# A two-block transformer layer on one core: loads in another order, own banks for two chunks, weigh products spread

## The reference, cut to what matters

```python
def first_block(x, mem, ...):
    h = rms_norm(x, g_mix_pre[l])
    proj = h @ w_in[l]                       # q, k, v of 8 + 8 heads of 64, forget gates
    o_f = fox_attention(...)                 # causal, with a decay from the forget gates
    o_c = chunked_rel_attention(...)         # chunks of 64, 8 to the left, relative bias
    mix = jnp.concatenate([rms_norm(o_f, ..), rms_norm(o_c, ..)], axis=-1) @ w_out[l]
    x = x + rms_norm(mix, g_mix_post[l])
    ca = memory_cross_attention(rms_norm(x, ..), rms_norm(mem, ..), w_mem_q[l], w_mem_kv[l], w_mem_o[l])
    x = x + rms_norm(ca, g_mem_post[l])
    x = x + rms_norm(swiglu(rms_norm(x, ..), w_gate_up[l], w_down[l]), g_ffn_post[l])

def second_block(x, c, ...):
    cond = jax.nn.silu(c)
    for l in range(2):
        ada = cond @ ada_w[l] + ada_b[l]     # shift, scale and gate, twice
        h = modulate(rmsnorm(x, norm_g[l, 0]), sh1, sc1)
        y = mlstm_mixer(h, ...) if l == 0 else mla_mixer(h, ..., *shared_kv)
        x = x + g1[:, None, :] * rmsnorm(y, norm_g[l, 1])
        h = modulate(rmsnorm(x, norm_g[l, 2]), sh2, sc2)
        y = sqrelu_mlp(h, mlp_w1[l], mlp_w2[l])
        x = x + g2[:, None, :] * rmsnorm(y, norm_g[l, 3])
```

## Time and profile before

| | |
|---|---|
| runs | 2259.11, 2255.01, 2258.81 us |
| median | 2258.81 us |
| profiled execution | 2257.02 us |
| its span in the trace | 2255.2 us |
| mean granted clock | 0.973 |
| PE busy | 2127.5 us (94%) |
| DVE, ACT, POOL busy | 1087.3, 876.0, 958.2 us |

### The profile page before, as it was taken

One profiled execution on the slowest core, in us unless ns is written; L12 is line 12 of the kernel. 1 busy time (PEld: TensorE's weight loads), 2 busy tenths in 40 slices (PEclk: granted clock), 3 DMA queues, 4 the chain that ended last, 5 costly groups with the idle time before them and its releaser, 6 DMA issues.

```text
span 2255.2 us, 27272 instructions
## 1 busy us (share of the span) xinstructions
PE 2127.5 (94%) x9534; PEld 1693.5 (75%) x9534; DVE 1087.3 (48%) x1672; ACT 876.0 (39%) x1442; POOL 958.2 (42%) x489
## 2 busy tenths in 40 slices
PE   5899889889999999889998999999999999999997
PEld 3777678677788888667766688888777776888886
DVE  2753661422465556655364543343565425343435
ACT  4224774344422222424265423222465544232332
POOL 2335676353344444423313344444435533444443
PEclk8999999999999999999999999999998999999999
DMA  4671034112254454347102223323222012233322
GB/s 172 211 266 45 20 116 146 57 37 75 66 179 159 156 171 164 112 159 262 65 1 69 67 84 95 101 93 95 91 78 72 1 47 66 88 98 93 100 95 84
DMA packets 66607, 234.38 MB, mean 104 GB/s; under 512 B 7136, under 2 KB 8416, under 8 KB 66400
## 3 DMA queue, kind: packets, MB, share of 16 engines
q1 hardware_dynamic: 66528, 233.33, 31.7%
HBM read 231.20 MB, written 2.10 MB: 103 GB/s over the span
## 4 chain that ended last, share of the span: by engine, by line
PE 72%; issue 13%; DVE 5%; ACT 5%; POOL 4%; DMA 1%; POOLq 0%; SPq 0%; DVEq 0%; ACTq 0%
PE bank L776 22%; PE bank L777 21%; PE bank L778 21%; POOL WL L658 3%; PE bank L883 2%; PE bank L868 1%; PE bank L950 1%; DVE H L2006 1%; DVE bank L2012 1%; PE bank L1017 1%; DVE Y L2248 0%; ACT Y L1556 0%; PE bank L889 0%; PE bank L1051 0%; PE bank L1276 0%
## 5 line engine op out<-in xcount | busy, mean ns | idle before, releaser
L658 POOL TENSOR_TENSOR WL<-stage,WH 128x1024 fp32r<-128x1024 f32 x272 | 660.6, 2429 | 1028.2 <-ACT WH L1378 1028.1
L1378 ACT ACTIVATE WH<-stage 128x1024 fp32r<-128x1024 f32 x272 | 288.2, 1060 | 918.6 <-PE bank L778 881.0
L776 PE MATMUL bank<-H,WH 128*128 128x512 f32 x1324 | 522.0, 394 | 25.3 <-DVE H L2006 11.8
L777 PE MATMUL bank<-H,WH 128*128 128x512 f32 x1324 | 519.4, 392 | 0.0
L778 PE MATMUL bank<-H,WL 128*128 128x512 f32 x1324 | 518.9, 392 | 0.0
L776 PEld LDWEIGHTS bank<-H,WH 128*128 128x128 f32 x1324 | 250.8, 189 | 84.9 <-issue 30.6
L778 PEld LDWEIGHTS bank<-H,WL 128*128 128x128 f32 x1324 | 250.8, 189 | 52.6
L777 PEld LDWEIGHTS bank<-H,WH 128*128 128x128 f32 x1324 | 250.9, 190 | 52.1 <-issue 0.5
L776 PE MATMUL bank<-HID,WH 128*128 128x512 f32 x688 | 268.8, 391 | 5.4 <-DVE Y L2248 5.4
L2248 DVE TENSOR_TENSOR Y<-bank,Y 128x512 f32<-128x512 f32 x344 | 226.3, 685 | 97.3 <-PE bank L778 96.4
L778 PE MATMUL bank<-HID,WL 128*128 128x512 f32 x688 | 268.4, 390 | 0.0
(11 more groups left out here) (394 smaller groups left out, 3075.8 us busy)
## 6 DMA issues: line engine op xcount, KB each, us to landing
stage<-panels SPq DMA_DIRECT2D x296, 512.0 KB, 3.5
apiece<-ada SPq DMA_DIRECT2D x112, 512.0 KB, 4.3
RAW<-panels SPq DMA_DIRECT2D x18, 512.0 KB, 3.8
x<-xT SPq DMA_DIRECT2D x4, 1024.0 KB, 7.8
outT<-x SPq DMA_DIRECT2D x8, 256.0 KB, 2.0
Y<-bias SPq DMA_DIRECT2D x1, 1024.0 KB, 4.8
V<-memT SPq DMA_DIRECT2D x2, 512.0 KB, 4.5
con<-cons SPq DMA_DIRECT2D x1, 517.0 KB, 6.7
```

The lines of the kernel that those rows point to most:

```text
L658: pool.tensor_tensor(low_of(p, slot), stage[:, slot, :], high_of(p, slot).bitcast(F32), ALU.subtract).then_inc(s_split, 1)
L776: pe.matmul(out, wh, rh, start=start, stop=False)
L777: pe.matmul(out, wh, rl, start=False, stop=False)
L1378: act.activation(high_of(p, slot), stage[:, slot, :], ACT.Copy).then_inc(s_hisplit, 1)
```

## The change

1. Start. x comes in three parts, the ones (a part of `con`) right behind the first of them with a semaphore of their own, and panels 0 and 1 before the rest of the constants, the condition and the gate weights. PE's mean square waits for the ones alone. ACT's high halves of panels 2 and 3 stand between its high chunks of x. SiLU of the condition and its table loads stand after the evacuation of chunk 0, and DVE waits for them after the low half of chunk 0.
2. SP's order of panels and pieces in w_in, a_in and the feed forward: panels first (`pieces_ahead`), pieces behind.
3. `own_bank`: chunks 2 and 3 of w_in, mem_q and a_in go to the banks ST and AD.
4. Self attention: weigh products by the table `WEIGHED_AT` over seven steps; ACT's outputs and value stage at steps 6 and 7, POOL's low half of the values at 7, four norm steps by one later.
5. mlp0 and mlp1: even groups in G[0] and G[1], odd ones in ST and AD, with waits relaxed by one group.
6. `warm(AD, 12)`, twelve matmuls whose result isn't used, ahead of the mla attention.
7. mem_q: high halves of its first panels between the squares of x, those of the extra ones between the high chunks.
8. Feed forward on DVE: pieces 0 to 3 right behind the first hidden values, then 4 of them behind each group's additions, and none in the last loop half.

```diff
+X_PARTS = [range(0, 2), range(2, 4), range(4, 8)]
+WEIGHED_AT = [[(0, 0), (0, 1)], [(1, 0), (1, 1)], [], [(0, 2)], [(1, 2)], [(0, 3)], [(1, 3)], []]
...
+        def own_bank(name, c):
+
+            return [ST, AD][c - 2] if name in JOINT and c in (2, 3) else G[c % 2]
...
+            for at, part in enumerate(X_PARTS):
+                sp.dma_start(x[:, part.start:part.stop, :],
+                             xT[part.start * P:part.stop * P, :].rearrange("(c p) t -> p c t", p=P))\
+                    .then_inc(s_x[at], 16)
+                if at == 0:
+                    sp.dma_start(con[:, 0:CON["mask"]], cons[:, 0:CON["mask"]]).then_inc(s_ones, 16)
             sp.dma_start(vec[:], vecs).then_inc(s_const, 16)
+            for slot in range(2):
+                sp.dma_start(stage[:, slot, :], panels[slot]).then_inc(s_stage[slot], 16)
...
+            def pieces_ahead(p0, q0, n):
 
                 with sp.Fori(0, n) as i:
                     for j in range(4):
-                        load_panel(i * 4 + (p0 + j), j % 2)
                         load_piece(i * 8 + (q0 + 2 * j), 0)
                         load_piece(i * 8 + (q0 + 2 * j + 1), 1)
+                        load_panel(i * 4 + (p0 + j), j % 2)
...
-            plain(p0, p0 + 12)
-            load_piece(q0, 0)
-            load_piece(q0 + 1, 1)
-            with sp.Fori(0, 4) as i:
-                for half in range(2):
-                    for j in range(6):
-                        load_panel(i * 12 + (p0 + 12 + 6 * half + j), j % 2)
-                        if j < 4:
-                            load_piece(i * 8 + (q0 + 2 + 4 * half + j), j % 2)
-            for j in range(6):
-                load_panel(p0 + 60 + j, j % 2)
-                if j < 4:
-                    load_piece(q0 + 34 + j, j % 2)
-            load_piece(q0 + 38, 0)
-            load_piece(q0 + 39, 1)
+            plain(p0, p0 + 6)
+            with sp.Fori(0, 10) as i:
+                for j in range(6):
+                    load_panel(i * 6 + (p0 + 6 + j), j % 2)
+                    if j < 4:
+                        load_piece(i * 4 + (q0 + j), j % 2)
             plain(p0 + 66, p0 + 68)
             p0, q0 = PANEL0["a_in"], 80
-            plain(p0 + 2, p0 + 4)
-            load_piece(q0, 0)
-            load_piece(q0 + 1, 1)
-            with_pieces(p0 + 4, q0 + 2, 3)
-            end_pieces(p0 + 16, q0 + 26, 8)
+            plain(p0 + 2, p0 + 6)
+            pieces_ahead(p0 + 6, q0, 3)
...
-                        if s >= 12 and s % 8 in (4, 5):
+                        if s >= 12 and s % 8 in (6, 7):
                             out(2 * (s // 8 - 1) + s % 2)
...
+                            if not gated and not (isinstance(g, int) and g < 2):
+                                pe.wait_ge(sm["hidden"], g * 2 + j - 3)
...
+            warm(AD, 12)
...
+                if c == 0:
+                    act.wait_ge(s_c, 16)
+                    act.activation(cond[:], cond[:], ACT.Silu).then_inc(s_cond, 1)
+                    load_ln_exp()
...
+                if m in (2, 5):
+                    act.wait_ge(s_used, RING1 - 1 + (m - 2) // 3)
+                    extra_high("mem_q", (m - 2) // 3)
...
-                hidden(0, 0)
-                with dve.Fori(0, (groups - 1) // 2) as i:
+                def two_groups(i, pieces_then):
                     hidden(i * 2 + 1, 1)
                     add(i * 2)
-                    pieces(i, 0)
+                    pieces(i, range(4, 8))
                     hidden(i * 2 + 2, 0)
                     add(i * 2 + 1)
-                    pieces(i, 1)
+                    if pieces_then:
+                        pieces(i, range(8, 12))
...
+                hidden(0, 0)
+                pieces(0, range(0, 4))
```

More of the change, by code:

```diff
@@ L978, in attention @@
                             score_pair(s + 4)
-                        if s >= 8 and s % 8 < 4:
-                            n, piece = 2 * (s // 8 - 1) + s % 2, s % 8 // 2 * 2
-                            weigh(n, piece)
-                            weigh(n, piece + 1)
+                        if s >= 8:
+                            for h, piece in WEIGHED_AT[s % 8]:
+                                weigh(2 * (s // 8 - 1) + h, piece)
                         continue
@@ L989, in attention @@
                 if name == "self":
-                    for half in range(2):
-                        for n in (heads - 2, heads - 1):
-                            weigh(n, 2 * half)
-                            weigh(n, 2 * half + 1)
+                    for step in WEIGHED_AT:
+                        for h, piece in step:
+                            weigh(heads - 2 + h, piece)
                 else:
@@ L1055, in feed_forward @@
                 sm = ff[name]
-                banks = [G[0], G[1], ST, AD] if gated else [G[0], None, G[1], None]
                 per = 2 if gated else 1
@@ L1589, in feed_forward @@
                 sm = ff[name]
-                banks = [G[0], None, ST, None] if gated else [G[0], None, G[1], None]
                 per = 2 if gated else 1
@@ L1663, in _ @@
             act.wait_ge(s_eps, 1)
-            squares("x", xc, lambda m: act.wait_ge(s_x if m < 4 else s_x2, 16))
+            squares("x", xc, lambda m: [act.wait_ge(s_x[at], 16) for at, part in enumerate(X_PARTS) if part.start == m])
             panel_high(0, 0)
@@ L1667, in _ @@
             root("x")
+            act.wait_ge(s_ones, 16)
             act.wait_ge(s_const, 32)
-            extra_high("w_in", 0)
-            high("x", scaled_in, hh, lambda m: col("zero"))
-            extra_high("w_in", 1)
+            for m in range(KC):
+                high_chunk("x", m, scaled_in, hh, lambda m: col("zero"))
+                if m in (4, 6):
+                    extra_high("w_in", (m - 4) // 2)
             act.activation(identr[:], ident, ACT.Copy)
```

103 lines of the change are left out of this document (55 added, 48 removed).

## The result

The changed kernel took 2283.4 us (median of 4 runs, 2280.5 to 2294.8) against 2259.0 of the kernel before (2255.0 to 2262.4): a ratio of 1.0118, with an interval of 1.0080 to 1.0157. It is 1.2% slower. The forecast was 2273, the range 2246 to 2296. The profiled execution after took 2284.55 us with a span of 2282.8, 27.6 more than the span of before.

The account below looks back on a forecast made before the run. TensorE, busy 94% of the span, bounds the kernel, so only its idle time or clock matters. Terms 59 - 7 - 7 - 9.6 + 4 - 8 - 9.3 - 8 = +14 on 2257.0 gave 2271, 2273 as median; range 2246 to 2296.

Parts of the forecast that it names:

- the feed forward's order: Feed forward loop: pieces behind later panels delay the down products, 4.2 us idle ten times (42) plus 17 of clock: +59.
- its tail: Feed forward's last loop half has no pieces, so 5.42 us of idle time and 1.6 of clock go: -7.
- a_in: Projection a_in: four waits and clock go (-11.8), two stalls of 5.9 and 7 with clock come (15.9): net +4.
- Rival (d): Projections: idle moves from chunks 2 and 3 to 4 and 5, only the start gains; 2285, no separate chance.
- mem_q: Projection mem_q: earlier high halves take away 7.33 us of idle time and 2.3 of clock: -9.6.
- The chain in the feed forward: With T the start of group h+1's products: late piece, hidden product T+20.9, low half T+25.8, down products needing it at T+21.76.
- Rival (a): Feed forward: the order costs nothing, as the hidden product may start as late as T+16.7; 2214, chance 0.13.
- The start: Before w_in: early ones and panels let the first products start at about 21.1 instead of 29.86 us: -8.7.
- w_in: Projection w_in: at best -26.8 including the start, but VectorE's remaining work returns 14.2 and some 5 of clock: -7.
- the MLPs: The two ungated MLPs: a second pair of banks ends a 2.80 us wait in each, with clock: -9.3 together.
- the self attention: Self attention: spread weigh products and moved steps cover about 1.3 us in each of six to seven units: -8.
- mla: Before mla attention: twelve extra products fill 2.39 us idle; the 20.48 us half-clock stretch, not all TensorE-bound, shortens: -8.

Follow-up runs that it names:

- The run at T+15.7: Changed kernel with the feed forward's pieces on SP one panel earlier (piece 4h+j behind panel 6h+5+j): 2222.9 us, ratio 0.9831.

## Why the prediction was right, and where it was not

**Sign and size.** Slower was right, and the measured 2283 lies 10 above the 2273 and inside the forecast's own 2260 to 2288. The reason given first is the right one: the feed forward's order, named as +59 with its tail at -7, measured +54.0 together. The spans differ by 27.6 us where the sum had 14. Nearly all of the difference is one term, a_in, which came out 15.8 higher; that the time still fell into the range is owed to the width of the range. Rival (d), the idle time moving to chunk 4, gave 2285, nearer than the forecast. That is what happened in a_in. But its +12 is the gain of a_in alone; the 9.6 of mem_q, which by its words should be gone too, is not in the sum, and mem_q kept its gain. So its nearness is luck.

**The chain in the feed forward** held step by step. In the group shown: issue of the panel T+14.8 (T+14.8 forecast), hidden product T+20.9 (T+20.9), down products T+25.7 (T+25.8 to 26.0). The ten idle times are 3.75 to 4.40 us, 39.4 in all (42). What it rested on was a row of the kernel before that showed the time at which the very panel is issued, and the fact that the hidden product of before stood directly behind its last piece with no room. Each of the ten idle times had its own slow stretch, and none stands in the loop without them. That bears out the rule of the Trainium skill (page "TensorE: Matmul & The Clock Gate", section "HAM oscillation — how this bites in real kernels"), by which the clock falls in every tile that waits. Their price was mis-sized low: seven stretches are 3.41 us long and three 6.83, 44.4 in all. 54.0 less the idle time of 39.4, plus the 5.4 of the tail, leaves about 20 for the clock net of the tail's own, and I had 17 less 1.6.

**Rival (a)** put the point from which the order decides at T+16.7 for the hidden product. The run at T+15.7 has no idle time, and the change at T+20.9 has 3.8, which fits a threshold at about T+17; no run lies between the two.

**The start** gave 10.8 instead of 8.7: the products start at 19.05, since the panels were split sooner than my 21.1, for which the prediction gives no working. No run takes the start alone.

**w_in** was right in its sum (+1.4 behind the start) and in the step that the work of VectorE is not gone. Its parts were not: idle times of 5.6, 1.7, 1.0, 2.7 and 2.2 us stand at chunks 4, 6, 8, 9 and 12, 13.2 in all where I had 14.2. Chunks 4, 8 and 12 were named, 6 and 9 not, and the sizes are other ones, so the sum is right in part by luck.

**mem_q, the MLPs, the self attention** came within 2 us. In each MLP the idle time of 2.8 us and its slow stretch are gone; the pair of banks is the only one of the eight changes that touches these stages, but no run takes it alone. The cause for mem_q was wrong in the prediction: "earlier high halves" were named, and the run with own banks alone shows that the banks do it. What is missing to 9.6 is an idle time of 1.7 us that the prediction didn't have, at 391.68, among the products of the memory values, where TensorE waits for VectorE's `acc`. One of 1.6 to 1.8 us stands there in every kernel built on the change, and in neither the kernel before nor the two built on it. For the self attention the run with it alone gave more (14.2 in the stretch) than it did within the change (8.4). The idle time fell alike, by 8.7 and 9.1 us; the difference is in the stretches at half clock, 17.1 us in the change as in the kernel before, and 3.4 in that run.

**mla** gave 11.0, not 8. The step that was mis-sized is that only part of the 20.48 us is bound by TensorE. 59 matmuls against 110 in the same time show that nearly all of it was: the stretch was worth 9.1. The rest are shorter stretches at half clock, 8.1 us in the stage before and 3.4 after.

**a_in** is the term that was wrong: +4 forecast, +19.8 measured, outside its bound of +10. The failed step is the one by which its four waits, 8.3 us, and 3.4 of clock go, the -11.8. Own banks don't take the wait away, they move it to chunk 4. With own banks and the old order the stage took 182.4 us (on the kernel before) and 180.0 (on the changed one), against 180.4: the -11.8 measured about 0. The prediction had seen this for w_in and rival (d) had said it, but the sum for a_in took the best case. The other part, the order, was forecast at +15.9 and measured +20.2. Its two stalls (5.9 and 7) are there, with 6.40 and 6.49. What was missed is the one behind the last pieces:

```profile
1117.92 1.23 DVE L2079 SCALAR_TENSOR_TENSOR apiece<-apiece,cond 128x1024 f32<-128x1024 f32 x1 [2.65 <-DMA apiece<-ada]
...
1121.44 0.23 ACT L1660 ACTIVATE gw<-gw 128x32 f32<-128x32 f32 x1 [11.84 <-DVE gw L2117]
...
1122.95 4.67 POOL L656 TENSOR_TENSOR WL<-stage,WH 128x1024 fp32r<-128x1024 f32 x2 [10.41 <-ACT WH L1381]
```

VectorE's last piece lands late, its gate operations stand behind it, ScalarE waits for them in order with two panel_high behind, and GpSimd's low half reaches TensorE with 5.37 us. In idle time and clock the same account reads: idle time forecast at +4.6 and measured +13.4, of which 3.48 at chunk 4 and 5.37 here were not in the sum; clock forecast at -0.4 and measured at about +6.4, with 20.5 us more at half speed.

## What to carry to other kernels

When transfers for two consumers share one in-order queue, moving one stream back for the sake of the other has a threshold: count, in units of the main loop, how much slack the displaced stream's last consumer has, because an engine in order passes a late product on to all that stands behind it. Ask of a new buffer not only whose wait it removes, but what the next user of the old one waits for; if the producer of that event has a backlog, the wait moves and doesn't shrink, as in w_in and a_in; if it has none, as in mem_q, the wait goes. And where TensorE must stand idle for two microseconds ahead of a long stretch of short products, look at the clock behind it: filling the idle time with products whose result isn't used was worth 9 to 11 us here.

## What the runs showed of the hardware

A stretch of 20.48 us at half clock behind 2.4 us of idle time was removed by twelve extra matmuls in the idle time, and came back without them. In that stretch it is nearly the clock alone that sets the rate: 59 against 110 matmuls. An idle time of about 2 us does not always have such a stretch behind it: at the head of the self attention every kernel built on the change has idle times of 2.19 and 1.6 us. In the changed kernel two stretches of 6.83 us at half clock go with them, in the run with pieces two panels earlier none. Of ten idle times of nearly the same length (3.75 to 4.40 us) in identical loop turns, seven were followed by 3.41 us at half clock and three by 6.83. The length of the idle time doesn't separate them (3.86, 3.88 and 4.10 us ahead of the long ones, 4.40 ahead of a short one). What does in this trace is when the clock fell: 0.86 to 1.30 us before the products resumed in the three long ones, from 0.46 before to 0.73 after in the seven short ones.
